# Recurrent block: the remainders of the first three outputs follow the scans of blocks 4, 5 and 6 on VectorE

## The chip, the core and the metric

The kernel runs on one core of a Trainium2 chip. The time is device microseconds of one execution. A core has a matmul engine (TensorE, PE in the rows; PEld is its weight load), VectorE (DVE), ScalarE (ACT) and GpSimd (POOL), each with its own instruction stream, which it works off in order. They meet through semaphores. SyncE (SP) issues the transfers from memory. TensorE has two clock levels, 1.2 and 2.4 GHz; views print the granted one as a share of the full one.

## The reference

A model of four layers on 256 tokens of width 1024 in float32: attention with convolution and a dense FFN; the recurrent mixer with a mixture of 8 experts; then two layers of three-branch mixers with dense FFNs. The change lies in the recurrent mixer:

```python
y_branch, x_branch = jnp.split(h @ w_in, 2, axis=-1)
y_branch = jax.nn.gelu(y_branch)
xc = causal_depthwise_conv(x_branch, conv_w) + conv_b
r = sigmoid(per_head(xc, ga_w) + ga_b);  i = sigmoid(per_head(xc, gx_w) + gx_b)
log_a = -8.0 * r * softplus(-lam)
a = exp(log_a);  b = sqrt(-expm1(2 * log_a)) * (i * xc)
_, hs = lax.associative_scan(combine, (a, b), axis=1)     # h[t] = a[t] * h[t-1] + b[t]
return (y_branch * hs) @ w_out
```

## The kernel before

**Precision.** Every float32 matmul is made of three in a shorter format: each operand is split into a high part (a cast) and a remainder (operand minus high part), and high x high, high x low and low x high are summed in the same bank of PSUM (L941 to L943 for the usual form). Weights come in pieces of 128 x 1024. For each piece j, SyncE loads it into a ring of 13 buffers `RAW` (with 6 more, `XRAW`, from the experts on), ScalarE casts it to `WHR` (L2276), VectorE writes the remainder `RAWR` over it (L1521). SyncE fills the `XRAW` buffers only once `rOLO[7]` is written (L770), since they lie on memory of the recurrent block.

**The recurrent block.** Its 1024 channels are 8 blocks m = 0 to 7 of 128 channels, with the 256 tokens along the free dimension. The stages on TensorE are "rx0" and "rx" (x branch), "ry" (y branch; block m is summed in bank B(m mod 4)) and then "ro", the projection with `w_out`. "ro" has 8 weight pieces, one for each block m. Its sums are four banks, B0 to B3 (2 halves of tokens x 2 halves of columns), so a piece means 4 groups of 3 matmuls. Pieces 0 to 3 run one after the other, each on all four banks. Pieces 4 to 7 then finish bank after bank. For block m, a matmul needs `rOHI[m]` (high part) and `rOLO[m]` (remainder); the wait on `rOLO[m]` stands ahead of the piece's first matmul. The first use of each bank also waits until the gelu of `ry` block 4, 5, 6 or 7 (L2490, ScalarE) has emptied it.

**The steps of block m at the end.** VectorE: `rI` = (a + 1) times the gated input (L1775), then the scan `rX` (L1776). GpSimd: `rY` times `rX` (L888). ScalarE: the cast of that product to `rOHI` (L2474). VectorE: the subtract `rOLO = rY - rOHI` (L1779).

**What sets the order.** The program is written for each engine apart, by generators that run along a common count of weight groups ("ticks"): `yield from skip(n)` lets n ticks pass. Small functions give the ticks of block m, counted from the start of "rx": `RN(m) = 64 + 2m` for the scans, and `RO(m)`, which is 75 to 79 for blocks 0 to 4 and 90, 97 and 108 for 5 to 7, for the end. The subtract stands at tick `RO(m) + 2`. "ro" begins at tick 96. The ticks only fix the order of instructions on each engine; when they run is set by semaphores. A remainder of a weight piece is written some ticks ahead of its first use, in between.

**After "ro".** VectorE adds each finished bank into X (L1580). ScalarE squares the sum (L2287), GpSimd takes the power -1/2 (L862), VectorE scales (L1547, `XN`), TensorE transposes (L967) and the result is split into `XHI` and `XLO` for the routing and the experts. For the first 128 tokens these transposes stand in TensorE's stream in the middle of the last bank of "ro" but one matmul group. Between the last subtract and the first two additions VectorE writes the remainders of the experts' first four weight pieces.

Of the kernel before, what the change touches and what calls it, by code (L numbers as in the profile page):

```python
# [117 lines left out]
def skip(n):  # L118
    for _ in range(n):
        yield False  # L120
# [28 lines left out]
def program(nc, A, out):  # L149
    with ExitStack() as ctx:  # L150
# [180 lines left out]
        def par(c, n=1):  # L331
            return PAR[:, c:c + n]
# [4 lines left out]
        def R(t):  # L337
            return t.bitcast(F32)
# [399 lines left out]
        def RC(m):  # L738
            return 11 + 4 * m
# [7 lines left out]
        def RN(m):  # L747
            return 64 + 2 * m
# [3 lines left out]

        def RO(m):
            return 75 + 1 * m if m < 5 else (90, 97, 108)[m - 5]

        def NS(u):
            return 169 + 4 * u if u < 4 else 187 + 6 * (u - 4)
# [102 lines left out]
        def gpsimd(e):  # L860
# [16 lines left out]
            def gated(m):  # L877
                yield from skip(RC(m) + 26)
                e.wait_ge(*rsig.of(m, 1))
                e.tensor_tensor(rI[:, m, :], rI[:, m, :], rC[:, m, :], ALU.mult).then_inc(*ri.by(m))  # L880
                yield from skip(RS(m) + 6 - RC(m) - 17)
                e.wait_ge(*rsq.of(m))
                e.wait_ge(*ri.of(m))
                e.tensor_tensor(rI[:, m, 1:256], rI[:, m, 1:256], rM[:, m, 1:256], ALU.mult).then_inc(*rp.by(m))
                yield from skip(RO(m) - RS(m) - 7)
                e.wait_ge(*(rgl if m < 4 else ryv).of(m))
                e.wait_ge(*rsc.of(m))
                e.tensor_tensor(rY[:, m, :], rY[:, m, :], rX[:, m, 0:256], ALU.mult).then_inc(*rp2.by(m))  # L888
# [624 lines left out]
        def vector(e):  # L1513
# [17 lines left out]
            def after(i):  # L1531

                i.then_inc(*dve.by())
                e.wait_ge(*dve.of())
# [228 lines left out]
            def r_channel(m):  # L1763
                yield from skip(RC(m))
                e.wait_ge(*rc0.of(m))
                for k in (1, 2, 3):
                    r = e.scalar_tensor_tensor(rC[:, m, :], rX[:, m, k:k + 256], par(P_RCW + m * 4 + k), rC[:, m, :],
                                               ALU.mult, ALU.add)
                    if k < 3:
                        after(r)  # L1770
                r.then_inc(*rc.by(m))
                yield from skip(RN(m) - RC(m))
                e.wait_ge(*rex.of(m))
                e.wait_ge(*rp.of(m))
                after(e.scalar_tensor_tensor(rI[:, m, 1:256], rR[:, m, 1:256], 1.0, rI[:, m, 1:256], ALU.add, ALU.mult))  # L1775
                e.tensor_tensor_scan(rX[:, m, 0:256], rR[:, m, :], rI[:, m, :], 0.0, ALU.mult, ALU.add).then_inc(*rsc.by(m))  # L1776
                yield from skip(RO(m) + 2 - RN(m))
                e.wait_ge(*rhi.of(m))
                e.tensor_tensor(rOLO[:, m, :], rY[:, m, :], R(rOHI[:, m, :]), ALU.subtract).then_inc(*rlo.by(m))  # L1779

            def recur():
                run("rx0")
                e.wait_ge(*fin("rx0", 0))
                e.memset(rX[:, :, 0:3], 0.0).then_inc(*rz.by(0))
                for m in CH:
                    clock.start(r_channel(m))
                run("rx")
                run("ry")
                run("ro", on=resid("ro", 3, lambda t, h: t * 2 + h, last=0))
# [476 lines left out]
        def scalar(e):  # L2266
# [176 lines left out]
            def r_channel(m):  # L2443
# [22 lines left out]
                if m < 4:  # L2466
                    yield from skip(RG_(m) - RE(m))
                    e.wait_ge(*ryv.of(m))
                    e.activation(rY[:, m, :], rY[:, m, :], ACT.Gelu_apprx_tanh).then_inc(*rgl.by(m))
                    yield from skip(RO(m) + 4 - RG_(m))  # L2470
                else:
                    yield from skip(RO(m) + 4 - RE(m))
# [503 lines left out]
```

## Time and profile before

| | |
|---|---|
| median of 3 runs | 2373.09 us (2370.86 to 2374.25) |
| the profiled execution | 2372.9 us, of which the span of its trace 2371.1 us |
| TensorE busy | 2321.7 us, 98% of the span |
| VectorE busy | 1777.4 us, 75% |
| ScalarE busy | 1471.6 us, 62% |
| GpSimd busy | 44.5 us, 2% |
| DMA | 593 MB, 250 GB/s on average |

All times of the trace are microseconds from the span's start. The recurrent block's end lies between 385 and 430 us, the routing up to 448, the experts from there to about 1430. A row of a timeline gives the start, the duration (of all its instructions, where it ends in "x2" or more), the engine, the line, and what is written from what; in brackets, the idle time ahead of it and what ended that.

### The profile page before, as it was taken

The numbers are of one execution on the slowest core, as the hardware profiler recorded it, in microseconds if no ns is written. First come the engines' busy times: TensorE is split into PE (matmuls) and PEld (weight loads), VectorE is DVE, ScalarE is ACT, GpSimd is POOL, SyncE is SP. The second block draws the span as 40 slices with busy tenths as digits, with TensorE's granted clock in tenths as the row PEclk, the third lists the DMA queues.
The fourth block names the chain that finished last, engine by engine and source line by source line (L and its number), as shares of the span: only waits on it lengthen the run. The fifth ranks groups of instructions, "written<-read, shape, count | busy, mean of one in ns | idle before, by whom it ended". The sixth has DMA issues, their size and how long they took to land.

```text
span 2371.1 us, 30689 instructions
## 1 busy us (share of the span) xinstructions
PE 2321.7 (98%) x11350; PEld 1920.0 (81%) x11350; DVE 1777.4 (75%) x2433; ACT 1471.6 (62%) x2025; POOL 44.5 (2%) x56
## 2 busy tenths in 40 slices
PE   8999998999999999999999999999999999999998
PEld 7888888788888888888888887877888888778887
DVE  7765557699988898989899896877755567777553
ACT  5554439487777777777777775665454456655442
POOL 0000003000000000000000000000000000000000
PEclk9999999899999999999999999999999999999999
DMA  7465554699999999999999995644565556345552
GB/s 281 139 207 187 187 177 151 237 356 368 364 340 359 369 366 336 362 356 374 345 355 374 362 335 193 222 134 131 180 211 184 177 179 222 108 148 180 190 183 80
DMA packets 164170, 593.29 MB, mean 250 GB/s; under 512 B 18480, under 2 KB 19248, under 8 KB 163888
## 3 DMA queue, kind: packets, MB, share of 16 engines
q1 hardware_dynamic: 164016, 591.27, 70.6%
q8 instruction: 93, 1.52, 0.3%
q14 instruction: 61, 0.50, 0.1%
HBM read 590.15 MB, written 1.05 MB: 249 GB/s over the span
## 4 chain that ended last, share of the span: by engine, by line
PE 92%; DVE 4%; ACT 2%; issue 1%; DMA 0%; POOL 0%; SPq 0%; DVEq 0%; POOLq 0%; ACTq 0%
PE B L941 27%; PE B L943 27%; PE B L942 27%; PE B L967 4%; DVE RAWR L1521 1%; ACT WHR L2276 1%; PE B L958 1%; PE B L959 1%; PE B L960 1%; PE B L1412 1%; PE B L1158 0%; PE B L1470 0%; PE B L1472 0%; PE B L1471 0%; PE B L1120 0%
## 5 line engine op out<-in xcount | busy, mean ns | idle before, releaser
L1521 DVE TENSOR_TENSOR RAWR<-RAW,WHR 128x1024 fp32r<-128x1024 f32 x894 | 1049.0, 1218 | 229.4 <-ACT WHR L2276 227.8
L2276 ACT CAST WHR<-RAW 128x1024 fp32r<-128x1024 f32 x894 | 902.0, 1047 | 170.8 <-PE B L943 162.8
L941 PE MATMUL B<-WHR,XHI 128*128 128x512 f32 (+2 forms) x1968 | 774.5, 394 | 2.2 <-DVE XLO L1559 1.4
L943 PE MATMUL B<-WHR,XLO 128*128 128x512 f32 (+2 forms) x1968 | 758.5, 385 | 0.0
L942 PE MATMUL B<-RAWR,XHI 128*128 128x512 f32 (+2 forms) x1684 | 646.5, 384 | 0.0
L943 PEld LDWEIGHTS B<-WHR,XLO 128*128 128x128 f32 x1968 | 370.5, 188 | 76.0
L941 PEld LDWEIGHTS B<-WHR,XHI 128*128 128x128 f32 x1968 | 371.4, 189 | 74.4 <-issue 2.3
L942 PEld LDWEIGHTS B<-RAWR,XHI 128*128 128x128 f32 x1684 | 318.1, 189 | 57.8
L1521 DVE TENSOR_TENSOR XRAWR<-XRAW,WHR 128x1024 fp32r<-128x1024 f32 x212 | 248.1, 1219 | 9.8 <-ACT WHR L2276 9.6
L2276 ACT CAST WHR<-XRAW 128x1024 fp32r<-128x1024 f32 x212 | 216.2, 1050 | 29.5 <-PE B L943 27.8
L941 PE MATMUL B<-WHR,mHI 128*128 128x512 f32 x448 | 177.0, 395 | 0.0
L943 PE MATMUL B<-WHR,mLO 128*128 128x512 f32 x448 | 176.0, 393 | 0.0
L942 PE MATMUL B<-RAWR,mHI 128*128 128x512 f32 x308 | 120.8, 392 | 0.0
L942 PE MATMUL B<-XRAWR,XHI 128*128 128x512 f32 x284 | 111.6, 393 | 0.0
L943 PEld LDWEIGHTS B<-WHR,mLO 128*128 128x128 f32 x448 | 84.2, 188 | 19.2
L941 PEld LDWEIGHTS B<-WHR,mHI 128*128 128x128 f32 x448 | 84.1, 188 | 18.1
L2586 ACT ACTIVATE mS<-B 128x512 f32<-128x512 f32 x56 | 33.5, 599 | 89.5 <-PE B L943 89.5
L1580 DVE TENSOR_TENSOR X<-X,B 128x512 f32<-128x512 f32 x60 | 40.9, 684 | 45.4 <-PE B L943 44.4
L943 PE MATMUL B<-WHR,ELO 128*128 128x512 f32 x176 | 69.3, 394 | 0.0
L942 PE MATMUL B<-RAWR,EHI 128*128 128x512 f32 x176 | 69.0, 392 | 0.0
L941 PE MATMUL B<-WHR,EHI 128*128 128x512 f32 x176 | 68.7, 390 | 0.0
L942 PEld LDWEIGHTS B<-RAWR,mHI 128*128 128x128 f32 x308 | 57.9, 188 | 12.0
(377 smaller groups left out, 2693.7 us busy)
## 6 DMA issues: line engine op xcount, KB each, us to landing
RAW<-in_m_u SPq DMA_DIRECT2D x155, 512.0 KB, 5.3
RAW<-in_m_d SPq DMA_DIRECT2D x154, 512.0 KB, 5.4
RAW<-in_m_g SPq DMA_DIRECT2D x151, 512.0 KB, 5.4
XRAW<-in_m_g SPq DMA_DIRECT2D x73, 512.0 KB, 5.3
XRAW<-in_m_d SPq DMA_DIRECT2D x70, 512.0 KB, 5.3
XRAW<-in_m_u SPq DMA_DIRECT2D x69, 512.0 KB, 5.2
RAW<-in_b_mg SPq DMA_DIRECT2D x48, 512.0 KB, 3.5
RAW<-in_b_g SPq DMA_DIRECT2D x44, 512.0 KB, 3.5
```

Source lines behind the costliest of these rows:

```text
L941: e.matmul(B[b][:, 0:w.n], lhsT=xh, rhs=wh, start=w.start, stop=False)
L942: e.matmul(B[b][:, 0:w.n], lhsT=xh, rhs=wl, start=False, stop=False)
L943: i = e.matmul(B[b][:, 0:w.n], lhsT=xl, rhs=wh, start=False, stop=w.fin)
L958: e.matmul(o, lhsT=wh, rhs=XHI[:, w.kt, :], start=w.start, stop=False)
L959: e.matmul(o, lhsT=wh, rhs=XLO[:, w.kt, :], start=False, stop=False)
L960: i = e.matmul(o, lhsT=wl, rhs=XHI[:, w.kt, :], start=False, stop=w.fin)
L967: r = e.transpose(B[b][:, tile(at + i)], s, ID)
L1412: r = e.matmul(B[7][64 * i:64 * i + 64, 0:128], lhsT=aVS[:, kb, b * 128 + g * 64:b * 128 + g * 64 + 64], rhs=aPT[:, q, tile(2 * i + c)], s ...
L1521: e.tensor_tensor(rawr(j)[:, 0:c], raw(j, c), R(WHI[:, j % NHI, 0:c]), ALU.subtract).then_inc(*lo.by(j))
L1580: return e.tensor_tensor(X[:, t, half(h)], X[:, t, half(h)], B[b][:, :], ALU.add)
L2276: e.copy(WHI[:, j % NHI, 0:c], raw(j, c)).then_inc(*hi.by(j))
L2586: e.activation(mS[:, cb % 2, :], B[mbank(x, cb, 0)][:, :], ACT.Silu).then_inc(*msl.by(x, cb))
```

## The change

The ticks of the subtracts of blocks 0, 1 and 2 on VectorE become 73, 75 and 77, in place of 77, 78 and 79. All others stay as they were.

```diff
+        def RL(m):
+            return 73 + 2 * m if m < 3 else RO(m) + 2
+
...
                 e.tensor_tensor_scan(rX[:, m, 0:256], rR[:, m, :], rI[:, m, :], 0.0, ALU.mult, ALU.add).then_inc(*rsc.by(m))
-                yield from skip(RO(m) + 2 - RN(m))
+                yield from skip(RL(m) - RN(m))
                 e.wait_ge(*rhi.of(m))
                 e.tensor_tensor(rOLO[:, m, :], rY[:, m, :], R(rOHI[:, m, :]), ALU.subtract).then_inc(*rlo.by(m))
```

The new function makes the line numbers after it larger by 3. Only VectorE's stream is changed. On VectorE, from block 4 on to the remainder of "ro"'s weight piece 2, the kernel before has this order (`rI` and `rX` are a block's two scan steps, here of blocks 4 to 7):

```order
L1775 SCALAR_TENSOR_TENSOR rI<-rR,rI 128x255 [waits rp,rex]
L1776 SCALAR_TENSOR_TENSOR rX<-rR,rI 128x256 [waits dve_steps]
L1775 SCALAR_TENSOR_TENSOR rI<-rR,rI 128x255 [waits rp,rex]
L1776 SCALAR_TENSOR_TENSOR rX<-rR,rI 128x256 [waits dve_steps]
L1775 SCALAR_TENSOR_TENSOR rI<-rR,rI 128x255 [waits rp,rex]
L1776 SCALAR_TENSOR_TENSOR rX<-rR,rI 128x256 [waits dve_steps]
L1779 TENSOR_TENSOR rOLO<-rY,rOHI 128x256 [waits rhi] x2
L1775 SCALAR_TENSOR_TENSOR rI<-rR,rI 128x255 [waits rp,rex]
L1776 SCALAR_TENSOR_TENSOR rX<-rR,rI 128x256 [waits dve_steps]
L1779 TENSOR_TENSOR rOLO<-rY,rOHI 128x256 [waits rhi]
L1521 TENSOR_TENSOR RAWR<-RAW,WHR 128x1024 [waits hi]
```

The same place with the change:

```order
L1778 SCALAR_TENSOR_TENSOR rI<-rR,rI 128x255 [waits rp,rex]
L1779 SCALAR_TENSOR_TENSOR rX<-rR,rI 128x256 [waits dve_steps]
L1782 TENSOR_TENSOR rOLO<-rY,rOHI 128x256 [waits rhi]
L1778 SCALAR_TENSOR_TENSOR rI<-rR,rI 128x255 [waits rp,rex]
L1779 SCALAR_TENSOR_TENSOR rX<-rR,rI 128x256 [waits dve_steps]
L1782 TENSOR_TENSOR rOLO<-rY,rOHI 128x256 [waits rhi]
L1778 SCALAR_TENSOR_TENSOR rI<-rR,rI 128x255 [waits rp,rex]
L1779 SCALAR_TENSOR_TENSOR rX<-rR,rI 128x256 [waits dve_steps]
L1782 TENSOR_TENSOR rOLO<-rY,rOHI 128x256 [waits rhi]
L1778 SCALAR_TENSOR_TENSOR rI<-rR,rI 128x255 [waits rp,rex]
L1779 SCALAR_TENSOR_TENSOR rX<-rR,rI 128x256 [waits dve_steps]
L1524 TENSOR_TENSOR RAWR<-RAW,WHR 128x1024 [waits hi]
```

The two subtracts between scan 6 and scan 7, and the one behind scan 7, now stand one each behind scans 4, 5 and 6. What follows on VectorE up to the additions into X is, with the change (before, the same, with L1521, L1779 and L1580 for the lines):

```order
L1782 TENSOR_TENSOR rOLO<-rY,rOHI 128x256 [waits rhi] x2
L1524 TENSOR_TENSOR RAWR<-RAW,WHR 128x1024 [waits hi]
L1782 TENSOR_TENSOR rOLO<-rY,rOHI 128x256 [waits rhi]
L1524 TENSOR_TENSOR RAWR<-RAW,WHR 128x1024 [waits hi]
L1782 TENSOR_TENSOR rOLO<-rY,rOHI 128x256 [waits rhi]
L1524 TENSOR_TENSOR RAWR<-RAW,WHR 128x1024 [waits hi] x3
L1782 TENSOR_TENSOR rOLO<-rY,rOHI 128x256 [waits rhi]
L1524 TENSOR_TENSOR RAWR<-RAW,WHR 128x1024 [waits hi] x4
L1583 TENSOR_TENSOR X<-X,B 128x512 [waits lin] x2
```

These are the subtracts of blocks 3 to 7, the remainders of "ro"'s pieces 3 to 7 and of the experts' first four pieces, and the first two additions. Nothing moved here.

## Rows read from the trace of the kernel before

**Rows 1.** Busy time by stretch: stretch, length, busy us of each engine, PEclk, DMA.
```profile
500.00:1400.00 900.00, 899.45 (x4100) 740.48 (x4099) 810.09 (x800) 689.85 (x757) 0.00 (x0) 1.00 0.97 360
```

**Rows 2.** Chain of waits, 395 to 436 us: start, us, what.
```profile
398.21 6.09 issue
...
429.86 0.70 DVE X L1580
...
432.97 0.81 PE B L967 x4
```

**Rows 3.** Timeline of VectorE, 396.5 to 406.3 us: scan 4, then scan 6.
```profile
398.93 1.10 DVE L1776 TENSOR_TENSOR_SCAN rX<-rR,rI 128x256 f32<-128x256 f32 x1
399.94 0.88 DVE L1775 SCALAR_TENSOR_TENSOR rI<-rR,rI 128x255 f32<-128x255 f32 x1
...
402.79 1.09 DVE L1776 TENSOR_TENSOR_SCAN rX<-rR,rI 128x256 f32<-128x256 f32 x1
```

**Rows 4.** Timeline of VectorE, the subtracts of blocks 0 and 1 apart.
```profile
403.81 0.39 DVE L1779 TENSOR_TENSOR rOLO<-rY,rOHI 128x256 fp32r<-128x256 f32 x1
...
404.13 0.94 DVE L1779 TENSOR_TENSOR rOLO<-rY,rOHI 128x256 fp32r<-128x256 f32 x1
```

**Rows 5.** Timeline of ScalarE: casts of blocks 0 to 3, the gelu of block 7.
```profile
399.72 0.40 ACT L2474 CAST rOHI<-rY 128x256 fp32r<-128x256 f32 x1
...
400.96 1.02 ACT L2474 CAST rOHI<-rY 128x256 fp32r<-128x256 f32 x3
...
404.34 0.38 ACT L2490 ACTIVATE rY<-B 128x256 f32<-128x256 f32 x1
```

**Rows 6.** Timeline of GpSimd, 397 to 408 us: the eight products.
```profile
397.50 5.83 POOL L888 TENSOR_TENSOR rY<-rY,rX 128x256 f32<-128x256 f32 x6 [3.69 <-ACT rY L2469]
404.03 0.76 POOL L888 TENSOR_TENSOR rY<-rY,rX 128x256 f32<-128x256 f32 x1 [0.69 <-DVE rX L1776]
406.27 0.76 POOL L888 TENSOR_TENSOR rY<-rY,rX 128x256 f32<-128x256 f32 x1 [1.49 <-DVE rX L1776]
```

**Rows 7.** Timeline of TensorE: piece 1 of "ro" begins; the first transposes.
```profile
409.52 0.40 PE L941 MATMUL B<-WHR,rOHI 128*128 128x512 f32 x1
...
426.70 0.60 PE L967 MATMUL B<-CST,XN 128*128 128x128 f32 x4
```

**Rows 8.** Timeline of VectorE, 406 to 424 us: remainders and the first additions.
```profile
406.37 1.75 DVE L1521 TENSOR_TENSOR RAWR<-RAW,WHR 128x1024 fp32r<-128x1024 f32 x1
...
415.40 4.62 DVE L1521 TENSOR_TENSOR RAWR<-RAW,WHR 128x1024 fp32r<-128x1024 f32 x4
420.72 0.69 DVE L1580 TENSOR_TENSOR X<-X,B 128x512 f32<-128x512 f32 x1 [0.70 <-PE B L943]
423.46 0.69 DVE L1580 TENSOR_TENSOR X<-X,B 128x512 f32<-128x512 f32 x1 [2.06 <-PE B L943]
```

**Rows 9.** Busy time by stretch again; PEclk is the third number from the end.
```profile
404.30:409.40 5.10, 5.10 (x12) 4.04 (x13) 5.07 (x8) 4.50 (x7) 1.25 (x2) 0.50 0.01 2
429.00:447.00 18.00, 13.65 (x71) 12.75 (x70) 8.90 (x38) 3.49 (x10) 0.55 (x1) 0.62 0.34 132
1565.00:1570.00 5.00, 5.00 (x30) 4.25 (x29) 3.87 (x23) 4.23 (x17) 0.00 (x0) 1.00 0.09 15
2024.00:2027.00 3.00, 3.00 (x13) 2.60 (x13) 1.56 (x8) 2.31 (x10) 0.00 (x0) 0.50 0.00 0
```

**Rows 10.** Timeline of TensorE: two other idle times of 2.9 us.
```profile
1564.41 1.05 PE L1374 MATMUL B<-CM,aQT 128*128 128x32 f32 x8 [2.92 <-ACT CM L2693]
...
2023.65 1.61 PE L1374 MATMUL B<-CM,aQT 128*128 128x32 f32 x8 [2.93 <-ACT CM L2693]
```

**Rows 11.** Timeline of SyncE's queue, and ScalarE's first cast from an extra buffer.
```profile
415.51 1.28 SPq L771 DMA_DIRECT2D XRAW<-in_m_u  x3
...
428.02 22.62 SPq L771 DMA_DIRECT2D RAW<-in_m_g  x4
...
450.48 1.03 ACT L2276 CAST WHR<-XRAW 128x1024 fp32r<-128x1024 f32 x1
```

## The prediction

> **What bounds the kernel now.** I read the busy time by stretch first. Between 500 and 1400 us TensorE is busy practically all the time [rows 1]: time is won only where TensorE stands still or runs slowly, and a delay there is paid in full. The chain of waits then shows the hole this change touches. TensorE does nothing for 6.09 us ahead of 404.30, the first matmul of the output projection "ro" [rows 2]. The view calls this "issue", so what it waited for is read from the code and the other engines. That matmul (L941) asks for four things: the cast and the remainder of weight piece 0 (written long before), bank B0 emptied, and `rOLO[0]`, the low half of output block 0.
>
> VectorE writes `rOLO[0]` at L1779, in program order behind the scans of blocks 4, 5 and 6. Scan 4 starts at 398.93, scan 6 at 402.79 [rows 3], then subtract 0 runs from 403.81 to 404.20 [rows 4], and TensorE starts 0.10 us later. Its source `rOHI[0]` was cast by ScalarE at 399.72 for 0.40 us, so it lay ready at 400.12 [rows 5]. The wait is one of order, not of data: 3.7 us lie between the two.
>
> **What is moved.** Nothing is added or removed: the same 8 subtracts run. Number 0 goes from behind scan 6 to behind scan 4, number 1 from behind scan 6 to behind scan 5, number 2 from behind scan 7 to behind scan 6. No DMA moves, and the queues of ScalarE, GpSimd, TensorE and SyncE keep their order.
>
> **Step 1, subtract 0.** Behind scan 4 VectorE is free at 399.94 (the start of the next row) [rows 3]. It waits for `rOHI[0]` to 400.12, with hand-over to about 400.2. How long the subtract takes there is bounded by two rows: 0.39 us where GpSimd stands still, 0.94 us where GpSimd multiplies beside it [rows 4]. GpSimd is at work without a break from 397.50 to 403.33 [rows 6], so I take 0.94: it ends at 401.1, and TensorE starts at 401.2 instead of 404.30, 3.1 us earlier, after an idle time of 3.0 us.
>
> **Step 2, the rest of weight piece 0.** Each piece is 4 groups of 3 matmuls, on banks B0 to B3. TensorE's next obstacle is new: B3 must have been emptied by the gelu of block 7, and ScalarE does that from 404.34 to 404.72 [rows 5]. Three groups need 9 x 0.229 = 2.1 us, to 403.3 (0.229 is 426.70 - 409.52 = 17.18 us over the 75 matmuls between) [rows 7]. So group 4 waits until 404.8 and piece 0 ends at 405.5. Before, piece 1 started at 409.52 [rows 7]: TensorE is now **4.0 us** ahead. Of these, 3.1 are the earlier start; the rest comes because piece 0 ran at half clock in 5.2 us [rows 9] and now does not, unless the clock falls again (rival B). From the trace of before, nothing in that gelu's way moves: it stands behind the cast of `rOHI[5]`, which needs scan 5 and a product of 0.76 to 0.98 us on GpSimd. Scan 5 now ends near 402.9, its product near 403.9, and ScalarE comes to that cast at 404.03 anyway.
>
> **Step 3, the scans behind the moved subtracts.** Scan 7 had subtracts 0 and 1 ahead of it and now has 2 as well. That is 0.4 to 0.9 us, plus the wait of 0.2 from step 1, less what scans and subtracts no longer lose where GpSimd now waits for scan 5 itself. I put scan 7 half a microsecond later. But the weight remainder behind it (406.37, 1.75 us, slowed by GpSimd's last product at 406.27) [rows 6, 8] no longer has subtract 2 ahead of it. So from there on VectorE's whole row is late by the wait and the contention alone: I take 0.1 us, with bounds of -0.2 (GpSimd idles in more of the stretch) and +0.8 (two more subtracts at 0.94 instead of 0.4, less 0.3 of the idle). That remainder is the one of piece 2: done at 408.2, and TensorE comes for it at 405.5 + 12 x 0.229 = 408.25. It just fits.
>
> **Step 4, where VectorE becomes the bound.** From 396.8 VectorE has no idle time until the four weight remainders that start at 415.40 and end at 420.02 [rows 8]. Only behind those stand the two additions into X (L1580) that begin the next norm. Before, they started at 420.72 and 423.46 because TensorE's sums came so late [rows 8]. Now TensorE has the sums 4.0 us earlier, at about 416.6 and 419.3, and the additions start when VectorE is through: the first at 420.1 (420.02 and the 0.1 of step 3), the second behind its 0.65, at 420.75. From the start of such an addition to the transposes of the normed half there are 432.97 - 429.86 = 3.11 us (add, square, GpSimd's power, scaling) [rows 2]. So the first transposes can start at 420.75 + 3.11 = **423.86**. Before they started at 426.70 [rows 7], and TensorE itself would be there at 426.70 - 4.0 = 422.7. It waits 1.15 us, and what is left of the 4.0 is 426.70 - 423.86 = **2.84 us**.
>
> **Step 5, does it reach the end?** Behind the transposes TensorE and VectorE run in the same pattern as before, all of it 2.8 us earlier: the end of "ro", the routing, the first expert. The weights could hold it up, since SyncE's queue waits for `rOLO[7]` before it fills the six extra buffers (415.51), and that moves later by the 0.1 of step 3 if at all. But the ring of buffers then fills up: the four issues from 428.02 on span 22.62 us, since the last of them waits for the first expert to free a buffer, and the first cast from an extra buffer comes at 450.48 [rows 11]: over 15 us of cover for a delay of under one. From there TensorE is the bound [rows 1] and nothing gives the time back.
>
> The sum: the profiled execution took 2372.9 us (span 2371.1), the median of the three runs is 2373.09, 0.2 above it. 2373.09 - 2.84 = **2370.25 us**.
>
> **A rule of the skill beside it.** Rows 4 show the same subtract at 0.39 us with GpSimd idle and at 0.94 beside it. The Trainium skill (SBUF — State Buffer, section "Who interferes with whom") says why: an instruction of VectorE with two SBUF inputs and a GpSimd instruction that reads SBUF hold each other off whole. By it the subtracts moved into GpSimd's busiest stretch also push GpSimd's products back, by up to 0.4 us each. Added in full to step 2 (0.8 us), the piece would end at 406.3 and TensorE would reach the transposes at 423.5, still ahead of 423.86: the sum stays, and only rival E is fed by it.
>
> **The rivals.**
> A, the forecast: VectorE's row is the bound in the end, gain 2.84, with 2.1 to 3.15 by the bounds of step 3. For it: four remainders without a gap ahead of the additions. 63%.
>
> B, the low clock stays on. Before, 6 us of idle time cost half clock for 5.1 us [rows 9]. Now there are 3.0 us of idle time, and a stretch of stop and go. Two idle times of that length stand in this trace: after 2.92 us at 1564.41 the clock stayed at 2.4 GHz, after 2.93 us at 2023.65 it was at 1.2 GHz [rows 9, 10]. So it is open. If it is low for 5.1 us from the start again, piece 0 ends at 401.2 + 5.1 = 406.3 (12 matmuls in 5.10 us at that clock), the transposes are reached at 423.5, and nothing is lost. If all of piece 1 is slow as well, it ends another 5.1 us on, at 411.4 instead of 408.25, and the gain is 426.70 - 425.85 = 0.85 us. In the middle, 1.7 us: 2371.4. 20%. The Trainium skill (TensorE: Matmul & The Clock Gate, Part 1) has the throttled state as the default, which activity releases; by it interrupted work is no sure way out, which feeds this rival.
>
> C, more comes back. TensorE's 4.0 us pass whole if VectorE's row is over a microsecond shorter than I think: 2369.1. Or the routing, where the clock is low for most of 18 us (0.62 of full on average) [rows 9], falls better: up to 3 us more. Against it: no row gives VectorE that microsecond. 8%.
>
> D, nothing happens: what ended the 6.09 us was not `rOLO[0]`, since the view itself says "issue". The four conditions above leave no other candidate near 404.2. 2373.1, 5%.
>
> E, slower. The one mechanism: VectorE takes its instructions in order, so while a moved subtract waits for its `rOHI` or for GpSimd, scans 5 to 7 wait behind it, then their products, the casts of `rOHI` 5 to 7, all weight remainders and the additions into X. It decides as soon as VectorE's row is late by more than 2.84 us at 420.02. Three subtracts at 0.94 instead of 0.4 make 1.6, the wait 0.2; another microsecond and more must come from waits for `rOHI` 1 and 2, which ScalarE casts from 400.96 on [rows 5], 1.5 us before VectorE asks. With a delay of 4 us: 2374.3. 4%.
>
> **How the numbers follow.** A holds most and gives 2370.25. Bounds of A are 2369.9 to 2371.0, B reaches to 2372.3; the three runs shown lie 3.4 us apart, so a median can stand a microsecond off on either side. Range 2368.1 to 2372.6, which leaves out most of D and E and C's upper half. A difference of 0.2%, about what a measurement of this kernel can tell from no change, is 4.75 us, and A, B and D stay below. Faster by more needs C's second half or a lucky sample: 0.07. Slower by more: 0.02. Within: 0.91.
>
> **What the changed kernel's profile would show.** Subtract 0 behind scan 4, near 400.2 and 0.9 us long (step 1). The idle time ahead of "ro" 3 us instead of 6.1. A second, short wait ahead of the first matmul on B3, ended by ScalarE's gelu near 404.7 (step 2). Piece 2's remainder done near 408.2 (step 3). No idle time of VectorE between the remainders and the additions into X, and a new wait of about 1.1 us of TensorE ahead of the transposes, ended by XN (step 4). The routing and everything after it earlier by 2.8 us (step 5). I am wrong if the first start doesn't move, if a granted clock of 0.5 lasts beyond 407, or if VectorE's four remainders end after 420.8.

## The result, and the profile after

| | median us | runs | ratio to before, 95% interval |
|---|---|---|---|
| kernel before | 2373.81 (2369.44 to 2377.80) | 19 | |
| changed kernel | 2369.20 (2366.44 to 2374.51) | 19 | 0.9982 (0.9976 to 0.9989) |
| changed kernel, a second comparison | 2370.75 (2365.41 to 2374.23) | 12 | 0.9990 (0.9981 to 0.9998) |

The changed kernel is faster by a little: its median is 4.6 us lower in the first comparison and 1.9 in the second (2372.67 for the kernel before), and both intervals end below 1. Over all runs of this study the means are 2370.12 (31 runs, standard error 0.45) for the changed kernel and 2373.24 (81 runs, 0.27) for the kernel before: a difference of 3.1 us, give or take 1.0. That is 0.13%, less than the 0.2% that the prediction took for the least difference a measurement of this kernel can tell, and the forecast said 2.84.

The profiled execution of the changed kernel took 2368.4 us (span 2366.6). VectorE, the rows that answer to [rows 3, 4 and 8]; line numbers are larger by 3:

```profile
399.20 1.10 DVE L1779 TENSOR_TENSOR_SCAN rX<-rR,rI 128x256 f32<-128x256 f32 x1
400.43 0.67 DVE L1782 TENSOR_TENSOR rOLO<-rY,rOHI 128x256 fp32r<-128x256 f32 x1
401.02 0.95 DVE L1778 SCALAR_TENSOR_TENSOR rI<-rR,rI 128x255 f32<-128x255 f32 x1
...
406.28 0.69 DVE L1779 TENSOR_TENSOR_SCAN rX<-rR,rI 128x256 f32<-128x256 f32 x1
406.89 1.20 DVE L1524 TENSOR_TENSOR RAWR<-RAW,WHR 128x1024 fp32r<-128x1024 f32 x1
...
415.91 4.61 DVE L1524 TENSOR_TENSOR RAWR<-RAW,WHR 128x1024 fp32r<-128x1024 f32 x4
420.45 1.27 DVE L1583 TENSOR_TENSOR X<-X,B 128x512 f32<-128x512 f32 x2
```

Subtract 0 stands behind scan 4 and starts at 400.43, when `rOHI[0]` is ready (cast from 400.00 to 400.40). At the end the two additions follow the four remainders without a gap, where before there were 0.70 and 2.06 us of idle time ahead of them [rows 8]. TensorE over the same place, then what it waited for between 400 and 430 us:

```profile
401.20 0.47 PE L944 MATMUL B<-WHR,rOHI 128*128 128x512 f32 x1 [2.73 <-issue]
...
403.35 0.50 PE L944 MATMUL B<-WHR,rOHI 128*128 128x512 f32 x1 [0.52 <-ACT rY L2493]
...
404.87 0.50 PE L944 MATMUL B<-WHR,rOHI 128*128 128x512 f32 x1 [0.56 <-ACT rY L2493]
...
424.16 0.66 PE L970 MATMUL B<-CST,XN 128*128 128x128 f32 x4 [0.90 <-DVE XN L1550]
```

```profile
PE B L944 <- issue: 2.7, 1, 2.7
PE B L944 <- ACT rY L2493: 1.1, 2, 0.6
PE B L970 <- DVE XN L1550: 0.9, 1, 0.9
```

The 6.09 us ahead of the projection [rows 2] are down to 2.73. Three new short waits appear: two for banks that ScalarE's gelu must empty first, and one of 0.90 us for XN, which is VectorE's row coming late. The view counts a wait from the end of the matmul before. Matmuls overlap, and start 0.23 us apart; so, had XN been ready, the transposes would have started 0.23 us behind the last matmul (422.86), at 423.09. They came 1.07 us later than that.

Busy time by stretch, 401 to 408 us of the changed kernel: the clock (third number from the end) stays at 1.00, where the kernel before had 0.50 for piece 0 [rows 9].

```profile
401.00:408.00 7.00, 5.72 (x22) 4.10 (x23) 6.90 (x10) 6.66 (x14) 4.01 (x5) 1.00 0.02 8
```

**A yardstick.** In the ten traces the recurrent block's last gate matmuls start up to 1.4 us apart. So I measure from the start of TensorE's last group of 4 gate matmuls, which nothing here touches, to the first transposes of XN. Of the kernel before and of the changed one:

```profile
377.51 1.13 PE L1082 MATMUL B<-rC,rW 128*128 128x256 f32 x4 [0.50 <-DVE rC L1767]
```

```profile
377.78 1.13 PE L1085 MATMUL B<-rC,rW 128*128 128x256 f32 x4 [0.49 <-DVE rC L1770]
```

Before: 426.70 [rows 7] - 377.51 = 49.19 us. After: 424.16 - 377.78 = 46.38. The change is worth **2.81 us** on this yardstick, where the forecast had 2.84.

### The profile page after: what moved, and what is told of

The parts are those of the page before. It is cut to its first block, busy times and chain, and to the rows that moved or that the text cites. A ratio compares the mean times of both kernels' runs of the same rounds, so it can differ in the third digit from the quotient of the medians.

```text
span 2366.6 us, 30689 instructions
## 1 busy us (share of the span) xinstructions
PE 2318.9 (98%) x11350; PEld 1917.0 (81%) x11350; DVE 1776.8 (75%) x2433; ACT 1471.1 (62%) x2025; POOL 44.8 (2%) x56
## 3 DMA queue, kind: packets, MB, share of 16 engines
HBM read 590.15 MB, written 1.05 MB: 250 GB/s over the span
## 4 chain that ended last, share of the span: by engine, by line
PE 90%; DVE 5%; ACT 3%; issue 2%; POOL 1%; DMA 0%; SPq 0%; DVEq 0%; POOLq 0%; ACTq 0%
PE B L944 27%; PE B L946 26%; PE B L945 26%; PE B L970 4%; DVE RAWR L1524 2%; ACT WHR L2279 1%; PE B L961 1%; PE B L1415 1%; PE B L962 1%; PE B L963 1%; PE B L1161 0%; PE B L1123 0%; PE B L1473 0%; PE B L1475 0%; PE B L1474 0%
```

## The experiments

Where an experiment adds lines, line numbers shift. All distances on the yardstick, each from one trace, with the mean granted clock from 401 to 408 us. In before and f4_adds_before this mean takes in the idle time ahead of the projection:

| kernel | subtract 0 starts | first addition starts | first transposes | TensorE's wait there | clock 401 to 408 |
|---|---|---|---|---|---|
| before | 26.30 | 43.21 | 49.19 | none | 0.62 (0.50 in piece 0) |
| changed | 22.65 | 42.67 | 46.38 | 0.90 | 1.00 |
| e1_again | 22.65 | 42.70 | 46.40 | 0.91 | 1.00 |
| e2_only0 | 22.65 | 42.55 | 46.25 | 0.77 | 1.00 |
| e3_warm_before | 26.38 | 42.53 | 46.88 | none | 1.00 |
| e4_adds_first | 22.64 | 41.31 | 47.41 | none | 0.52 |
| f1_adds_warm | 22.64 | 39.36 | 45.36 | none | 1.00 |
| f2_warm_after | 22.65 | 42.71 | 46.41 | 0.90 | 1.00 |
| f3_early0 | 22.64 | 43.33 | 47.67 | none | 0.58 |
| f4_adds_before | 26.30 | 43.48 | 49.46 | none | 0.63 |

### The changed kernel again (e1_again)

> The changed kernel once more, unaltered, to size the gain. Theory A (VectorE's row is the bound behind the output projection): 2.8 us under the kernel before, ratio 0.9988; transposes of XN near 424 us of the trace. Rival (a larger gain, 4.6 us as in the first comparison, because the shorter idle time also saves low clock elsewhere): ratio 0.9981, and the routing or the later mixers at full clock for longer in its trace.

Ratio 0.9990 (0.9981 to 0.9998), and 46.40 us on the yardstick against 46.38. The place that the change touches repeats within 0.02 us. The totals don't: the span of this sample is 2369.6 us, 3.0 more than the first. The rival's 4.6 us are not borne out at this place, and its routing is as slow as in the first trace (granted clock 0.66 from 430 to 450 us in both). The interval's lower end, 0.9981, just reaches them, so for the totals this sample alone rules nothing out. What moves the totals stands further below.

### Only subtract 0 moved (e2_only0)

```diff
-            return 73 + 2 * m if m < 3 else RO(m) + 2
+            return 73 if m == 0 else RO(m) + 2
```

> Only subtract 0 is moved (behind scan 4); subtracts 1 and 2 stand as in the kernel before. Theory A: subtract 0 alone carries the change. TensorE starts the projection at 401.2, weight piece 1 asks for rOLO[1] only at 405.7, when scan 6 and subtract 1 are over (about 405.2). Same time as the changed kernel within 0.3 us: ratio to before 0.9988. Rival (the moves of 1 and 2 count, since TensorE would otherwise wait for rOLO[1]): a new idle time of 0.5 us or more ahead of piece 1, and part of the gain lost.

Ratio 0.9988 (0.9980 to 0.9997), yardstick 46.25. No wait appears ahead of piece 1; piece 2 starts 0.14 us late, since its remainder is done only at 408.18, and that costs nothing. Subtract 0 alone carries the whole change; the other two moves give nothing, and cost 0.1 us of VectorE's row if anything (42.67 against 42.55).

### The clock alone (e3_warm_before)

```diff
             def recur():
...
+                e.wait_ge(*rsig.of(6, 1))
+                for _ in range(24):
+                    e.matmul(B[5][:, 0:512], lhsT=XHI[:, 0, 0:128], rhs=XHI[:, 0:2, :].rearrange("p a c -> p (a c)"), start=True, stop=True)
                 linear("ro", tiles(rOHI, rOLO), lambda kt, t: rlo.of(kt), lambda t, h: t * 2 + h,
```

> The kernel before, with 24 matmuls of 512 columns on data at hand, into the unused bank B5, in TensorE's idle time ahead of the projection (5.5 of the 6.09 us); the subtracts are not moved. It isolates the half clock that follows the idle time. Theory: piece 0 starts at 404.3 as before but takes 2.75 us in place of 5.2, so all behind it is 2.35 us earlier, which VectorE's row (through at 420.0, transposes possible from 423.8) still permits: ratio 0.9990. Rival (the clock costs nothing of its own, since VectorE would be late anyway): ratio 1.0000.

Ratio 0.9989 (0.9980 to 0.9998). Nothing of the order was touched, and TensorE starts the projection as late as before. Timeline of TensorE, then of VectorE:

```profile
404.85 0.47 PE L941 MATMUL B<-WHR,rOHI 128*128 128x512 f32 x1 [0.71 <-issue]
405.16 0.39 PE L942 MATMUL B<-RAWR,rOHI 128*128 128x512 f32 x1
...
424.85 0.60 PE L967 MATMUL B<-CST,XN 128*128 128x128 f32 x4
```

```profile
420.50 0.67 DVE L1583 TENSOR_TENSOR X<-X,B 128x512 f32<-128x512 f32 x1
421.62 0.69 DVE L1583 TENSOR_TENSOR X<-X,B 128x512 f32<-128x512 f32 x1 [0.44 <-PE B L943]
```

But the first matmuls take 0.47 and 0.39 us and not 0.77 and 0.63: the clock was at 2.4 GHz, and the transposes come 2.31 us earlier (46.88 against 49.19; 2.35 expected). So 2.3 of the 2.8 us can be had without moving a single subtract. The second addition still waits 0.44 us for TensorE, so here TensorE is the bound; VectorE was ready 0.44 us earlier.

### The additions ahead of the remainders (e4_adds_first)

```diff
-            def run(name, on=None, lead=4):
-                for w in groups[name]:
-                    rests(min(w.j + lead + 1, w.oldest + NHI, NP))
+            def run(name, on=None, lead=4, cap=None):
+                for i, w in enumerate(groups[name]):
+                    rests(min(w.j + lead + 1, w.oldest + NHI, NP, cap(i) if cap else NP))
...
-                run("ro", on=resid("ro", 3, lambda t, h: t * 2 + h, last=0))
+                run("ro", on=resid("ro", 3, lambda t, h: t * 2 + h, last=0), cap=lambda i: M0 + (0 if i < 20 else 2))
...
+                rests(M0 + 4)
                 m_split(0, 0, 4)
                 m_split(0, 1, 5)
```

(`M0` is the experts' first weight piece. The first addition now stands ahead of all four remainders, two follow it, then the second addition; the other two are written ahead of the first expert's split.)

> The changed kernel with the first two additions into X taken out from behind the remainders of the experts' first four weight pieces on VectorE: two remainders now stand between the two additions, two ahead of the first expert's split. Theory A (those four remainders are what holds the gain at 2.84 of 4.0 us): additions at about 416.9 and 419.6, TensorE's wait of 0.90 us ahead of the transposes goes, transposes at 423.1 in place of 424.16, about 1.1 us faster than the changed kernel; against before 4.0 us, ratio 0.9983. Rival (what TensorE waits for there is something else, or the remainders come back as a wait at the first expert): no faster than the changed kernel, or a new idle time near 446.

Ratio 0.9992 (0.9983 to 1.0001), and in the trace 47.41 us: a miss, 1.0 us slower than the changed kernel. The reason is rival B of the prediction, caught in this sample. TensorE's timeline and the clock:

```profile
401.22 0.54 PE L946 MATMUL B<-WHR,rOLO 128*128 128x512 f32 x1
402.12 0.79 PE L944 MATMUL B<-WHR,rOHI 128*128 128x512 f32 x1 [0.36 <-ACT rY L2496]
402.71 0.63 PE L945 MATMUL B<-RAWR,rOHI 128*128 128x512 f32 x1
...
408.08 0.42 PE L945 MATMUL B<-RAWR,rOHI 128*128 128x512 f32 x1
```

```profile
401.00:408.00 7.00, 6.63 (x16) 4.51 (x15) 6.93 (x11) 6.65 (x12) 3.45 (x4) 0.52 0.00 1
```

After the same idle time (2.72 us here, 2.73 in the changed kernel's sample) the clock went down 1.3 us into the work and stayed there to 408. The first addition then waited for TensorE:

```profile
417.87 0.69 DVE L1583 TENSOR_TENSOR X<-X,B 128x512 f32<-128x512 f32 x1 [3.13 <-PE B L946]
```

VectorE had nothing to do for 3.13 us; so its row is no longer the bound. This sample can't say what the addition's place is worth at full clock. The next one does.

### Additions ahead, and the clock held (f1_adds_warm)

The edits of e4_adds_first, and that of e3_warm_before with `range(11)`.

> The changed kernel with the additions into X ahead of the four remainders, and with 11 matmuls of 512 columns into the unused bank B5 (2.5 us) in TensorE's remaining idle time, so that its clock can't fall there. Distances are taken from the start of the last gate matmuls (the group of 4 at 377.5 in the kernel before) to the first transposes of XN: 49.2 us before, 46.4 with the change. Theory A and B together (VectorE's four remainders and the clock are the two things that hold the gain): 45.3 us, no wait of TensorE ahead of the transposes, ratio 0.9983 to before. Rival (the additions' place is worth nothing): 46.4 us.

Timeline of TensorE, then of VectorE:

```profile
398.01 2.68 PE L1097 MATMUL B<-XHI 128*128 128x512 f32 x11
400.94 0.47 PE L944 MATMUL B<-WHR,rOHI 128*128 128x512 f32 x1 [0.25 <-issue]
...
422.84 0.63 PE L970 MATMUL B<-CST,XN 128*128 128x128 f32 x4
```

```profile
416.84 0.69 DVE L1586 TENSOR_TENSOR X<-X,B 128x512 f32<-128x512 f32 x1 [1.11 <-PE B L946]
417.44 2.35 DVE L1527 TENSOR_TENSOR RAWR<-RAW,WHR 128x1024 fp32r<-128x1024 f32 x2
419.71 0.68 DVE L1586 TENSOR_TENSOR X<-X,B 128x512 f32<-128x512 f32 x1
```

45.36 us, as expected (45.3), and no wait ahead of the transposes: 3.83 us under the kernel before, 1.02 under the changed one. That is the 4.0 us TensorE was ahead by, nearly whole. Against f2_warm_after below, which holds the clock and leaves the additions where they were, it is 1.05 us (46.41), so this microsecond is the additions' place and not the clock. At the first expert it is still there: the matmuls that pick its tokens (mG times XN) start at 82.07 on the yardstick, in the changed kernel at 83.05. The total is another matter: ratio 0.9989 (0.9980 to 0.9998), no better than the changed kernel, where 0.9983 was expected. Eleven runs that spread over 6 us don't resolve one microsecond.

### The clock held in the changed kernel (f2_warm_after)

Only the 11 extra matmuls.

> The changed kernel with only the 11 extra matmuls in TensorE's idle time. Theory A: in a sample in which the clock doesn't fall they change nothing, 46.4 us from the gate matmuls to the transposes, since VectorE is the bound; over many runs they take away those in which it falls, ratio to before 0.9987 and a slightly lower median than the changed kernel. Rival (TensorE is the bound and any lost clock is paid in full): a distance under 46.4 us.

46.41 us with the same wait of 0.90 us for XN: where the clock doesn't fall by itself, holding it gives nothing, since VectorE is the bound. Ratio 0.9991 (0.9981 to 1.0001), where 0.9987 was expected; whether the median gains over many runs stays open, the interval is too wide.

### Subtract 0 too early (f3_early0)

```diff
-            return 73 + 2 * m if m < 3 else RO(m) + 2
+            return (72, 75, 77)[m] if m < 3 else RO(m) + 2
```

> The changed kernel with subtract 0 moved one step further up, in front of block 4's scan pair, where its source is not ready: VectorE must wait about 2.2 us for rOHI[0]. It measures rival E of the prediction, the price of a wait on VectorE with the scans queued behind it. Theory: TensorE starts no earlier (401.2), subtract 0 ends at about 401.0, scans 4 to 7 and all remainders come 1.9 us later (2.2 us of wait, less the 0.25 that subtract 0 waits in the changed kernel), the additions at 422.3, 48.2 us from the gate matmuls to the transposes in place of 46.4: ratio to before 0.9996. Rival (VectorE's row has slack, the wait is absorbed): 46.4 us.

Ratio 0.9995 (0.9985 to 1.0004). The wait is there, but VectorE's row pays only a third of it. VectorE:

```profile
399.60 0.87 DVE L1782 TENSOR_TENSOR rOLO<-rY,rOHI 128x256 fp32r<-128x256 f32 x1 [2.13 <-ACT rOHI L2477]
400.39 0.41 DVE L1778 SCALAR_TENSOR_TENSOR rI<-rR,rI 128x255 f32<-128x255 f32 x1
400.83 0.69 DVE L1779 TENSOR_TENSOR_SCAN rX<-rR,rI 128x256 f32<-128x256 f32 x1
```

GpSimd:

```profile
396.95 3.24 POOL L891 TENSOR_TENSOR rY<-rY,rX 128x256 f32<-128x256 f32 x4 [3.69 <-ACT rY L2472]
401.67 0.77 POOL L891 TENSOR_TENSOR rY<-rY,rX 128x256 f32<-128x256 f32 x1 [1.48 <-DVE rX L1779]
```

The first addition is at 43.33, 0.66 us later than in the changed kernel, where 1.9 was expected. While VectorE waited, GpSimd ran its four products faster (0.81 us each on average, 0.97 before [rows 6]) and was through. Then block 4's pair, which takes 0.95 and 1.10 us in the changed kernel, took 0.41 and 0.69, and the first step of block 5 took 0.40 where it takes 0.95. From start to start that is 1.5 us less for the three, against 0.2 more for subtract 0. The changed kernel waits 0.2 us for `rOHI[0]` too, so 1.9 us of the wait are new: 1.9 - 1.5 + 0.2 = 0.6, and 0.66 were measured. Most of the new wait replaced time that VectorE otherwise loses beside GpSimd.

The transposes stand at 47.67. VectorE's row alone would put them 0.66 us behind the changed kernel's 46.38, at 47.04. The rest comes from TensorE: the clock had again fallen here (0.58), and the second addition waits 0.42 us for it.

### Additions ahead in the kernel before (f4_adds_before)

The edits of e4_adds_first on the kernel before.

> The kernel before with only the additions into X moved ahead of the remainders. Theory A: TensorE, not VectorE, is the bound there, so nothing is gained: 49.2 us from the gate matmuls to the transposes, or 0.2 more since two remainders (2.3 us) now stand between the two additions, which lie 2.75 us apart. Rival (the order of the additions alone gives the gain): 48 us or less.

This kernel ran once, so it has a trace and no ratio. 49.46 us against 49.19: nothing is gained. VectorE waits 5.51 us ahead of the first addition, and the second is a little later for the two remainders between:

```profile
420.58 0.69 DVE L1580 TENSOR_TENSOR X<-X,B 128x512 f32<-128x512 f32 x1 [5.51 <-PE B L943]
421.19 2.35 DVE L1521 TENSOR_TENSOR RAWR<-RAW,WHR 128x1024 fp32r<-128x1024 f32 x2
423.45 0.68 DVE L1580 TENSOR_TENSOR X<-X,B 128x512 f32<-128x512 f32 x1
```

## Why the prediction was right, point by point

**Step 1, the start.** Right: idle time 2.73 us for 3.0 foretold, 3.37 us of movement for 3.1 (26.79 to 23.42 on the yardstick). Subtract 0 took 0.67 us, between the bounds of 0.39 and 0.94; I had taken the upper one. GpSimd multiplies without a break there (one row of five products from 397.78, 4.79 us), so it wasn't idle beside it.

**Step 2, the fourth bank.** Right in place and time: the gelu of block 7 at 404.43 with the group behind it at 404.87. I had missed that B2 makes TensorE wait too, 0.52 us; it costs nothing, since B3 comes later. That the moved subtracts would push GpSimd's products back, and this gelu with them, didn't happen: it stands at 26.65 on the yardstick, before at 26.83.

**Step 3, scans and remainders.** Right in the sum: on the yardstick the first addition starts at 42.67 us, where 420.1 - 377.51 = 42.59 was foretold. On the way the shares are others: piece 2's remainder is done 0.4 us earlier than I had put (408.09, 30.3 on the yardstick, for 30.7), since GpSimd's last product fell later and slowed the two subtracts behind it instead. The size is in part luck: the four remainders start 0.24 us later than before (38.13 against 37.89) where I had put 0.1, and the first addition starts 0.07 us before their row ends, which I hadn't reckoned with.

**Step 4, VectorE as the bound.** Right, and shown from both sides. The changed kernel has the wait for XN (0.90 us in the view, 1.07 counted from where the transposes could have started, for 1.15 foretold). f1_adds_warm takes the remainders away and the wait goes, with 1.02 us. f4_adds_before makes the same edit where TensorE is the bound, and it gives nothing. The size, 2.81 for 2.84, is a little better than its parts: TensorE could have been at the transposes at 423.09, 45.31 on the yardstick, which is 3.9 us ahead and not 4.0, and f1_adds_warm, where nothing holds it, has 45.36. Up to 416 us its matmuls are 0.233 us apart where I had taken 0.229; the traces don't say why.

**Step 5, the way to the end.** Right in kind: no wait for weights appears, the routing is 2.58 and the first expert 2.76 us earlier on the yardstick. What no step had were the differences of several microseconds from run to run. In the ten traces they lie in five places behind the gate matmuls; between these, distances agree within 0.2 us. The first is the one that the change does touch: the clock behind the idle time in the recurrent block (rival B), and the routing behind it, 35.6 to 37.2 us from the first transposes to the first expert. The second is an idle time inside the experts, near 1065 us, which is 0.55 us in the sample of before and 1.75 in e2_only0:

```profile
1067.02 0.47 PE L941 MATMUL B<-WHR,XHI 128*128 128x512 f32 x1 [0.55 <-issue]
```

```profile
1065.14 0.47 PE L944 MATMUL B<-WHR,XHI 128*128 128x512 f32 x1 [1.75 <-issue]
```

No wait is listed there in the changed kernel's trace, and f3_early0 has 2.43 us. What sets it wasn't tried. It matters for the sum: the eight traces that reach the first expert earlier have 0 to 2.43 us there, 1.2 on average, the two that reach it late (before and f4_adds_before) 0.55 and none. So some of the gain may be given back there; ten traces neither show nor exclude it.

The third is the stretch from the experts' end to the idle time in the first three-branch mixer, 127.7 us in e2_only0 and f2_warm_after and 129.2 to 130.3 in the others. The fourth is the clock behind that idle time of 2.9 us [rows 10], worth up to 3.2 us. The clock held in the samples of before and of the changed kernel, and from the start behind the idle time (L1377) to the mixer's next products (L1427) they take 76.52 us each. It fell in the eight others, and the same work takes 78.05 to 79.71. The changed kernel over 40 us there, then e1_again, the same kernel:

```profile
1560.00:1600.00 40.00, 38.47 (x234) 31.31 (x235) 32.30 (x118) 27.13 (x77) 0.00 (x0) 1.00 0.35 113
```

```profile
1560.00:1600.00 40.00, 37.08 (x205) 30.14 (x205) 30.45 (x115) 25.15 (x74) 0.00 (x0) 0.91 0.35 114
```

That alone makes e1_again 3.1 us slower than the first sample of the same kernel (79.65 against 76.52). The fifth is the clock after the idle time of 2.9 us in the second mixer [rows 10]. The kernel before over 15 us there, then the changed kernel over the same work:

```profile
2020.00:2035.00 15.00, 12.07 (x58) 9.91 (x57) 10.50 (x48) 8.73 (x26) 0.00 (x0) 0.77 0.23 70
```

```profile
2017.00:2032.00 15.00, 12.07 (x65) 9.94 (x64) 12.12 (x57) 9.73 (x30) 0.00 (x0) 0.89 0.22 70
```

The two profiled executions differ by 4.5 us in their spans. 3.0 of that are there at 1435 us, and 2.9 until 2020; the rest arose behind, in that stretch of lower clock, which was shorter this time. So the excess of this pair of traces over 2.8 us is luck. The 19 runs of each kernel have no traces, but every run of the changed kernel has its mean granted clock on record, and it fits: the mean is 0.9938 over the 19 runs of the first comparison and 0.9931 over the 12 of the second, and within each comparison the runs with a lower clock are the longer ones (correlation -0.72 and -0.65, where -1 would be a straight line). That points to low clock having been met less often in the first comparison's runs. It isn't shown run by run.

**The rivals.** B is real. After some 2.8 us of idle time the clock held in three samples (changed, e1_again, e2_only0) and fell in two (e4_adds_first, f3_early0). After 6 us, without the extra matmuls, it fell in both samples (before, f4_adds_before); with them it fell in none of three. The three and two are five traces of four kernels, and f3_early0 has a second idle time of 1.01 us behind the first. The two mixers' idle times of 2.9 us, which no kernel here touches, say more, though other work follows them: over the ten traces the clock fell after 8 of 10 in the first mixer and after 9 of 10 in the second. I had seen one of each in the kernel before and given B 20%; that was too low. Its price was about right: 49.19 - 47.41 = 1.8 us are left in e4_adds_first, where I had 1.7. D fell with e2_only0: moving subtract 0 alone moves TensorE's start. C's first half was made to happen by f1_adds_warm, by other means than a shorter row; its second half, the routing, isn't seen (2.58 us earlier, no more than the rest). E's mechanism is there (f3_early0), but its price was overrated: 2.13 us of waiting cost VectorE's row 0.66. Mis-sized was my bound of step 3 (up to 0.94 for each subtract): the three moved subtracts took 0.67, 0.39 and 0.40 us. It counts as new loss what VectorE and GpSimd lose to each other only once, whichever goes first. The Trainium skill (SBUF — State Buffer, "Who interferes with whom") describes an exclusive lock, under which whoever comes second waits the other's instruction out; by it the loss goes with the pairs that meet, and f3_early0, where the same instructions ran short once GpSimd was through, is in line with that.

## What to carry to other kernels

An engine's wait that the profile can't name may be one of program order on another engine: look up when the operand was written, when its source was ready, and what stands between the two. The gain of such a move is not the idle time removed (3.4 us here) but the distance to the next engine that becomes the bound (2.8), and half clock behind an idle time is a part of that price: holding the clock alone gave 2.3. Where runs of a kernel differ by more than the change is worth, measure from one untouched instruction to the first one behind the place, in every trace: here that repeats to 0.02 us between two traces of the same kernel with the clock held (46.38 and 46.40), and 31 runs of the whole program give 3.1 with 1.0 either way.

## What the runs showed that I had not expected

The clock can fall after the work has begun again. In e4_adds_first five matmuls of the projection ran at 2.4 GHz and the sixth (0.54 us) was caught by the change; it stayed at 1.2 GHz to 408, although TensorE paused for only 0.36 us more. In the changed kernel's sample, with an idle time of the same length (2.73 us), it didn't fall at all before the transposes. One trace in which the clock holds says little about the next: the largest difference between two traces of the same kernel, 3.1 us, came from one such idle time far from the change.

A wait on VectorE beside a busy GpSimd can cost far less than it lasts. The pair of instructions of block 4 took 0.95 and 1.10 us beside GpSimd's products and 0.41 and 0.69 after them (f3_early0), and of the 2.13 us waited only 0.66 arrived at the additions.
